# Weights kept across three stage seams: a second pass that begins with the last group, filler matmuls at the ends of stages, and fp32r splits shared out anew

## The chip, the cores and the metric

The kernel runs on one core of one Trainium2 chip. The metric is the device time in microseconds (us) of one launch. TensorE is called PE in the rows, VectorE DVE, ScalarE ACT, GpSimd POOL, SyncE SP (it only issues transfers). PEld is PE's weight load.

## The reference

One decoder layer is run over a prompt of 2048 tokens (width 1024) and over 8 single-token samples, all in fp32. What matters here:

```python
h = rmsnorm(x) @ w_in         # queries, keys, values, z of three branches and three gates, in groups of 512 columns
o_fox = fox_prompt(...)       # 8 heads x 64: softmax(q k^T * scale + c_t - c_s), causal, times v
o_hg, state = hgrn2(...)      # 4 heads x 128: gated linear recurrence, a state of 128x128 per head
o_mem = mem_attn(q, mk, mv)   # 4 heads x 128 over 256 memory tokens; mk, mv = rmsnorm(mem) @ w_mk, w_mv
ya, yb, ym = (o_fox*silu(z)) @ w_pa, (rmsnorm(o_hg)*silu(z)) @ w_pb, (o_mem*silu(z)) @ w_pm
y = rmsnorm(x + (sigmoid(ga)*ya + sigmoid(gb)*yb + sigmoid(gm)*ym) @ w_o)
```

The samples attend to a paged cache of 2048 past tokens each and have their own recurrent state. Keys, values, log gates, memory keys and values and states are outputs too.

## The kernel before

Six stages follow each other. Each is a block: all engines must have ended the one before they start the next.

1. `normalise_and_project`: norms of 16 prompt tiles of 128 tokens (and 2 memory tiles), turned by PE; the first group of columns, `hi`.
2. `project_and_decode`: seven groups (`DENSE`: fq, mq, hf, hq, hz, fz, mz) over two passes of the tokens. A pass keeps 8 of the 16 token tiles in `x_both`. A unit is one tick: 24 matmuls of 512 columns (8 slices of the contraction, 3 products each). A group is 8 ticks, so there are 14 groups and 112 ticks. The other 8 token tiles are loaded over the first during the last group of pass one. Beside it the samples' attention over their cache (`Decode`, laid out by tick numbers), their recurrence and the forget gates run.
3. `recur_prompt`: the recurrence, 64 chunks `n`; five lead-in steps (`AHEAD`) prepare the first units.
4. `attend_prompt`: forgetting attention, a hand-written list `steps`.
5. `attend_memory`.
6. `merge_and_finish`: branch projections, gates, `w_o`, final norm.

A product in fp32 is made of three fp32r matmuls: a number is split in a high part (a cast to fp32r) and a low part (number minus high part). For each weight slice of 128x512 somebody has to load a raw slice, cast it (`..._hi`) and subtract (`..._lo`). In stage 2 POOL does all three for all 104 slices (`split_slice`, with `RAWS` = 2 raw buffers); the slices live in a ring of 16 places (`ring_hi`, `ring_lo`), the last four of which serve the cache's values during decoding.

Ten column groups (fk, fv, six halves of gates, and mk, mv of the memory) are not done in stage 2: the `Filler` spreads their matmuls through stages 3 to 5, to keep PE at work while the others compute. `fill.begin` cuts them into slots: a group has 400 matmuls (16 tiles by 24, and 16 more for the samples), mk and mv have 48 each. A group's eight weight slices are split by POOL as soon as the last tile of the group before has used them (`Filler.split_slice`). Each tile of tokens comes by a load `fill_x` of 1 MB, two buffers. `MATMULS` sets the counts: 1600 in the recurrence (four whole groups, over 134 slots), 100 + 1396 in the attention, 200 in the memory stage.

PE, ACT, DVE and POOL run their own lists in order; a wait holds whatever stands behind it on that engine. At the start of stage 3 POOL builds the masks before it releases `consts`, for which PE and DVE wait; at the start of stage 4 PE waits for `consts_ready`. In stage 6 the 16 slices of `w_o` pass through the same four raw buffers as the branch weights: SP loads, ACT casts, DVE subtracts, all between tile 0's branches and its `mixed` turn.

## Time and profile before

| | us |
|---|---|
| median of 3 runs | 3064.44 (3054.81 to 3074.55) |
| the profiled execution | 3058.63 |
| its span, first to last instruction | 3056.9 |
| PE busy in the span | 2802.7 (92%) |
| DVE busy | 1583.8 (52%) |
| ACT busy | 1036.8 (34%) |
| POOL busy | 811.6 (27%) |
| mean granted PE clock | 0.961 |

Busy is the time in which an instruction of the engine ran. A group of rows with "[x <-y]" at the end of a row tells that the engine was idle for x us before that row's first instruction and that y ended the wait. The granted clock is 1.00 at 2.4 GHz and 0.50 at 1.2 GHz; a stretch's number is its mean.

### The profile page before, as it was taken

To read this page: it belongs to the slowest core of one execution; us is meant where nothing else is said; L and a number is where in the kernel's file an instruction comes from. 1 tells how busy PE (TensorE), PEld (TensorE's weight loads), DVE (VectorE), ACT (ScalarE), POOL (GpSimd) and SP (SyncE) were. 2 spreads that over 40 slices of the span, in tenths; PEclk is the share of its full clock that TensorE was granted. 3 is DMA by queue.
4 is the path that set the end of the run, shared out by engine and by line. 5 is a ranking of instruction groups with operands and counts; after the bars stand their busy time and mean duration, and the time that the engine had idled before them with its cause. 6 is when DMAs were issued, how large, how long until landed. Compare 5 with 4: busy or idle time off the path is not lost. (4 is left out here: it accounts for less than half of the span.)

```text
span 3056.9 us, 38630 instructions
## 1 busy us (share of the span) xinstructions
PE 2802.7 (92%) x13880; PEld 2295.1 (75%) x13880; DVE 1583.8 (52%) x3023; ACT 1036.8 (34%) x1972; POOL 811.6 (27%) x846
## 2 busy tenths in 40 slices
PE   7899998999995989999779999999999977999998
PEld 5678776667774878787658888888887865888887
DVE  5415676343443446556426665666664545444544
ACT  2211111332321334344225555555554234232322
POOL 6058885344244252533350020020020000000000
PEclk9999998999997999999889999999999998999999
DMA  5587778566544657666575455554443545433331
GB/s 168 222 257 230 233 249 277 186 176 185 174 136 143 200 194 244 205 219 200 176 223 155 138 147 160 156 160 142 139 139 114 198 170 173 131 107 117 116 109 49
DMA packets 292430, 528.44 MB, mean 173 GB/s; under 512 B 110398, under 2 KB 135551, under 8 KB 270991
## 3 DMA queue, kind: packets, MB, share of 16 engines
q1 hardware_dynamic: 239967, 408.13, 42.5%
q0 software_dynamic: 16656, 53.36, 6.0%
q10 hardware_dynamic: 35616, 64.47, 5.5%
q8 instruction: 111, 1.82, 0.2%
q14 instruction: 80, 0.66, 0.1%
HBM read 413.19 MB, written 112.68 MB: 172 GB/s over the span
## 5 line engine op out<-in xcount | busy, mean ns | idle before, releaser
L2452 PE MATMUL fill_out<-fill_w_hi,fill_x 128*128 128x512 f32 x2112 | 739.1, 414 | 94.3 <-POOL fill_w_lo L2545 45.0
L2452 PEld LDWEIGHTS fill_out<-fill_w_hi,fill_x 128*128 128x128 f32 x2112 | 393.7, 193 | 174.4 <-POOL fill_w_lo L2545 58.9
L2452 PE MATMUL fill_out<-fill_w_lo,fill_x 128*128 128x512 f32 x1056 | 438.1, 415 | 0.0
L461 DVE TENSOR_TENSOR fox_pt_lo<-fox_turned,fox_pt_hi 128x512 fp32r<-128x512 f32 (+1 forms) x320 | 194.8, 609 | 157.1 <-ACT fox_pt_hi L408 155.3
L2086 ACT ACTIVATE in_stage<-in_out 128x512 f32<-128x512 f32 (+1 forms) x119 | 70.9, 597 | 593.7 <-PE in_out L99 546.3
L408 ACT ACTIVATE fox_pt_hi<-fox_turned 128x512 fp32r<-128x512 f32 (+1 forms) x320 | 170.1, 531 | 300.8 <-PE fox_turned L358 299.1
L447 DVE CUSTOM_DVE_ANT_0 fox_probs<-fox_scores,fox_bias 128x512 f32<-128x512 f32 (+2 forms) x320 | 187.5, 608 | 93.1 <-PE fox_scores L347 50.6
L2543 POOL CAST fill_w_hi<-fill_raw 128x512 fp32r<-128x512 f32 x80 | 51.5, 644 | 678.5 <-PE fill_out L2463 643.5
L2452 PEld LDWEIGHTS fill_out<-fill_w_lo,fill_x 128*128 128x128 f32 x1056 | 204.6, 194 | 30.5
L97 PE MATMUL in_out<-x_first,ring_hi 128*128 128x512 f32 x512 | 201.0, 393 | 7.4 <-POOL ring_lo L2007 7.4
L99 PE MATMUL in_out<-x_first,ring_hi 128*128 128x512 f32 x512 | 200.5, 392 | 0.0
L98 PE MATMUL in_out<-x_first,ring_lo 128*128 128x512 f32 x512 | 200.5, 392 | 0.0
L358 PE MATMUL fox_turned<-ident,fox_probs 128*128 128x128 f32 x1088 | 172.7, 274 | 9.1 <-ACT fox_probs L399 8.9
L97 PE MATMUL mf_out<-mf_w_hi,mf_t_hi 128*128 128x512 f32 x408 | 166.4, 408 | 1.5 <-DVE mf_w_lo L2919 1.5
L99 PE MATMUL mf_out<-mf_w_lo,mf_t_hi 128*128 128x512 f32 x408 | 161.3, 395 | 0.0
L98 PE MATMUL mf_out<-mf_w_hi,mf_t_lo 128*128 128x512 f32 x408 | 161.1, 395 | 0.0
L358 PEld LDWEIGHTS fox_turned<-ident,fox_probs 128*128 128x128 f32 x1088 | 128.5, 140 | 39.4 <-ACT fox_probs L399 14.6
L97 PE MATMUL in_out<-ring_hi,x_first 128*128 128x512 f32 x384 | 154.1, 401 | 4.0 <-POOL ring_lo L2007 4.0
L399 ACT ACTIVATE fox_probs<-fox_probs,fox_neg_most 128x128 f32<-128x128 f32 (+15 forms) x128 | 153.2, 1197 | 11.4 <-ACT fill_stage L2479 9.3
L98 PE MATMUL in_out<-ring_hi,x_first 128*128 128x512 f32 x384 | 152.7, 398 | 0.0
L99 PE MATMUL in_out<-ring_lo,x_first 128*128 128x512 f32 x384 | 152.7, 398 | 0.0
L2007 POOL TENSOR_TENSOR ring_lo<-in_raw,ring_hi 128x512 fp32r<-128x512 f32 x104 | 146.7, 1410 | 8.7
(356 smaller groups left out, 5932.8 us busy)
## 6 DMA issues: line engine op xcount, KB each, us to landing
fill_x<-x_tiles SPq DMA_DIRECT2D x132, 1024.0 KB, 5.4
dc_slot<-in_cache_fox_k_dram SPq DMA_DIRECT2D x128, 256.0 KB, 3.9
dc_slot<-in_cache_fox_v_dram SPq DMA_DIRECT2D x128, 256.0 KB, 3.1
in_raw<-in_w_in_dram POOLq DMA_DIRECT2D x104, 256.0 KB, 4.0
plain<-fill_stage ACTq DMA_DIRECT2D x96, 256.0 KB, 5.4
mf_gate<-plain SPq DMA_DIRECT2D x96, 256.0 KB
turned<-in_stage ACTq DMA_DIRECT2D x64, 256.0 KB, 3.9
fill_raw<-in_w_in_dram POOLq DMA_DIRECT2D x64, 256.0 KB, 3.0
```

The costliest lines, as they stand in the source:

```text
L97: pe.matmul(out, a[0], b[0], start=first, stop=False)
L98: pe.matmul(out, a[1], b[0], start=False, stop=False)
L99: return pe.matmul(out, a[0], b[1], start=False, stop=last)
L358: last = pe.transpose(bank_of(st)[:, t * P:(t + 1) * P], probs_of(4 * q + t, j * P, (j + 1) * P), core.ident[:])
L399: act.activation(probs_of(i, 0, (i + 1) * P), probs_of(i, 0, (i + 1) * P), ACT.Exp, bias=neg_most[:, slot:slot + 1], accum_out=row_sum[:, ...
L408: act.activation(pt_hi[:, zeta % PT_SLOTS, skip:BANK], bank_of(st)[:, skip:BANK], ACT.Copy).then_inc(hi_ready, 1)
L447: dve.tensor_tensor_reduce(probs_of(i, c * BANK, c * BANK + width), scores[s % S_BANKS][:, 0:width], bias[:, c * BANK:c * BANK + width], 1 ...
L461: dve.tensor_tensor(pt_lo[:, b, skip:BANK], bank_of(st)[:, skip:BANK], pt_hi[:, b, skip:BANK].bitcast(F32), ALU.subtract).then_inc(turned_ ...
L2007: pool.tensor_tensor(lo, raw[m % RAWS][:], hi.bitcast(F32), ALU.subtract).then_inc(split, 1)
L2086: act.activation(stage[s][0:rows_, :], out[e % OUTS][0:rows_, :], how, scale=scale).then_inc(sigmoid_ready if kind == "silu" else taken, 1)
L2452: ins = pe.matmul(self.out[n % self.OUTS][:], x, w, start=(k == 0 and term == 0), stop=(ends and term == 2))
L2543: pool.tensor_copy(self.w_hi[:, k, :], self.raw[n % self.RAWS][:]).then_inc(self.split, 1)
```

## The change

- Pass two of stage 2 takes its groups in the order mz, fq, mq, hf, hq, hz, fz. The first of them is the group that pass one ended with, and its split weights stay where they are. Pass two waits for each token tile by itself.
- In place of the group that is no longer loaded, the first Filler group's weights (fk) are split at the end of stage 2, into the upper half of the ring. That half is now two tensors, `keep_hi` and `keep_lo`, which outlive stage 2 and serve the Filler as its weights.
- Casts in stage 2 go from POOL to ACT (`high`), and POOL keeps the loads and the subtractions (`low`). There are three raw buffers. In pass one two slices are taken per tick in ticks 0 to 3 of a group, where one per tick stood in ticks 0 to 7. In the recurrence the Filler's casts go to ACT as well.
- Ticks of the decode's softmax steps and of the forget gates move later by one to three.
- Stage 3: PE no longer waits for constants at its start, POOL builds the masks after the first unit's gates, SP loads the first token tile before anything else. 96 filler matmuls stand at the end, in four slots between the last output pieces.
- Stage 4: PE's wait for constants stands at the first score; head 1's queries and values are loaded later; 10 and 12 filler matmuls frame the last `back`. Stage 5 begins with 16 filler matmuls and has one more slot.
- The filler matmuls are shared out anew, and mk, mv come after the third gate half.
- Stage 6: POOL loads, casts and subtracts `w_o` through two buffers that are parts of `gains`; the final gain is loaded behind it.

The diff, cut to its core:

```diff
 attend_prompt
-    steps += [("out", *quads[-1]), ("back", *quads[-1])]
+    TAIL = FILLS + 2 * FH * J_HEAD
+    steps += [("out", *quads[-1]), ("fill", TAIL), ("back", *quads[-1]), ("fill", TAIL + 1)]
...
-                        if st[0] in ("queries", "values") and st[2] == QUADS - 1 and st[1] + 1 < FH:
+                        if st[0] in ("queries", "values") and st[2] == QUADS - 1 and 1 <= st[1] < FH - 1:
                             (load_queries if st[0] == "queries" else load_values)(st[1] + 1)
+                        if st == ("score", 0, 0, 0):
+                            load_queries(1)
+                            load_values(1)
...
-                pe.wait_ge(consts_ready, 1)
...
+                        if (h, i, c) == (0, 0, 0):
+                            pe.wait_ge(consts_ready, 1)
 recur_prompt
-        fill.begin([0] * 2 * SPLITS + fill.spread(matmuls, 2 * (len(chunks) + AHEAD - SPLITS)))
+        fill.begin(fill.spread(matmuls, 2 * (len(chunks) + AHEAD)) + fill.spread(last_matmuls, TAIL), True)
...
+                fill.sync_start(sp)
                 load_unit(0)
+                fill.sync_next(sp)
+                load_unit(1)
                 load_v(0)
-                fill.sync_start(sp)
-                for u in range(1, HH):
+                for u in range(2, HH):
                     load_unit(u)
...
-                    if n + AHEAD < SPLITS:
-                        fill.gpsimd_first(pool, n + AHEAD, SPLITS)
+                    if n == 2 - AHEAD:
+                        build_masks()
...
+                def tail(piece):
+                    for slot in tail_slots(piece):
+                        fill.tensor(pe, slot)
 attend_memory
-        fill.begin(fill.spread(matmuls, NT))
+        fill.begin([first_matmuls] + fill.spread(matmuls - first_matmuls, NT + 1))
...
+                fill.tensor(pe, 0)
                 pe.wait_ge(kv_loaded, 32)
 Decode.tensor
-            if m == 2:
+            if m == 3:
                 pe.wait_ge(self.spread_ready, a + 1)
 project_and_decode
+    group_at = [*range(G), G - 1, *range(G - 1)]
+    load_at = [n if n < G else n - 1 for n in range(N + 1)]
...
+        def split_at(m):
+            n, k = first_use[m // KT], m % KT
+            if ring_before[m] is not None and last_use[ring_before[m] // KT] == n - 1:
+                return n * U - 1
+            return (n - 1) * U + (k // 2 if n < G else k)
...
+                def low(m):
+                    hi, lo = w_ring.at(ring_at[m])
+                    pool.wait_ge(cast, m - KT + 1)
                     pool.tensor_tensor(lo, raw[m % RAWS][:], hi.bitcast(F32), ALU.subtract).then_inc(split, 1)
-                    if m + RAWS < N * KT:
-                        pool.wait_ge(split, 2 * (m - KT) + 2)
+                    if m + RAWS < SLICES:
+                        pool.wait_ge(split, m - KT + 1)
                         load_raw(m + RAWS)
...
-                    if n == G and u % 4 == 0:
-                        pe.wait_ge(x_loaded[u // 4], 64)
+                    if n == G:
+                        pe.wait_ge(x_loaded[u], 16)
...
+                def high(m):
+                    act.wait_ge(raw_loaded[m % RAWS], 16 * ((m - KT) // RAWS + 1))
+                    ring_free(act, m)
+                    act.activation(w_ring.at(ring_at[m])[0], raw[m % RAWS][:], ACT.Copy).then_inc(cast, 1)
+
                 for t in range(TICKS):
+                    for m in range(KT, SLICES):
+                        if split_at(m) == t and t % U == U - 1:
+                            high(m)
                     for e in events_at(t):
                         evict(e)
                         if e >= 1:
                             store(e - 1)
+                    for m in range(KT, SLICES):
+                        if split_at(m) == t and t % U < U - 1:
+                            high(m)
 Filler
+    def high_by_scalar(self, act, n):
+        self.wait_slice(act, n)
+        act.activation(self.w_hi[:, n % KT, :], self.raw[n % self.RAWS][:], ACT.Copy).then_inc(self.cast, 1)
 merge_and_finish
+            @block.gpsimd
+            def _(pool):
...
+                for i in range(2):
+                    load(i)
+                for i, (kk, n) in enumerate(last_slices):
+                    at = slice(n * BANK, (n + 1) * BANK)
+                    pool.wait_ge(late_loaded[i % 2], 16 * (i // 2 + 1))
+                    pool.tensor_copy(w_hi[:, kk, at], late_raw[i % 2]).then_inc(late_split, 1)
+                    pool.wait_ge(late_split, 2 * i + 1)
+                    pool.tensor_tensor(w_lo[:, kk, at], late_raw[i % 2], w_hi[:, kk, at].bitcast(F32), ALU.subtract
+                                       ).then_inc(late_split, 1)
+                    if i + 2 < len(last_slices):
+                        pool.wait_ge(late_split, 2 * i + 2)
+                        load(i + 2)
+                pool.wait_ge(late_split, 2 * len(last_slices))
+                pool.dma_start(gains[:], gain.partition_broadcast(P)).then_inc(gains_loaded, 16)
...
-                            pe.wait_ge(w_split, MERGE_W + (n + 1) * KT)
+                            pe.wait_ge(late_split, 2 * (n + 1) * KT)
-MATMULS = {"recur": 1600, "first": 100, "fox": 1396}
+MATMULS = {"recur": 1340, "recur_last": 96, "fox_first": 144, "fox": 1472, "fox_last": [10, 12], "memory_first": 16}
```

Three places in the order of the instructions. The first is POOL's list at the start of the recurrence; `fill_raw` are the Filler's raw slices, `hg_f0` the gates of unit 0. Before:

```order
L2529 DMA fill_raw1<-in_w_in_dram 128x512
L635 MEMSET hg_masks 128x512
...
L647 AFFINE_SELECT hg_masks<-hg_masks 128x128 x4
L649 MEMSET hg_state 128x512
L650 MEMSET hg_ones 128x128
L669 TENSOR_SCALAR hg_f0<-hg_f0,rest,bound 128x512
L672 TENSOR_SCALAR hg_k0<-hg_f0 128x512
L2543 CAST fill_w_hi<-fill_raw0 128x512
L2545 TENSOR_TENSOR fill_w_lo<-fill_raw0,fill_w_hi 128x512
L2529 DMA fill_raw0<-in_w_in_dram 128x512
...
L656 TENSOR_TENSOR hg_level0_0<-hg_b0 128x512
```

And with the change:

```order
L2611 DMA fill_raw1<-in_w_in_dram 128x512
L651 MEMSET hg_state 128x512
L652 MEMSET hg_ones 128x128
L688 TENSOR_SCALAR hg_f0<-hg_f0,rest,bound 128x512
L691 TENSOR_SCALAR hg_k0<-hg_f0 128x512
L675 TENSOR_TENSOR hg_level0_0<-hg_b0 128x512
...
L700 TENSOR_SCALAR hg_leaf_k0<-hg_leaf_k0 128x512
L656 MEMSET hg_masks 128x512
```

The masks stand behind unit 0's differences, and no weight slice is split here. The second place is PE's list at the end of the recurrence (`hg_kv` is the last chunk's update) and the start of the attention. Before:

```order
L846 MATMUL hg_o_sum0<-hg_state,hg_q_run3 128x128
L849 MATMUL hg_kv0<-hg_v1,hg_k_rows1 128x128
L572 UNCONDITIONAL_BRANCH
L303 UNCONDITIONAL_BRANCH
L2452 MATMUL fill_out0<-fill_w_hi,fill_x0 128x512 x2
```

With the change:

```order
L877 MATMUL hg_o_sum0<-hg_state,hg_q_run3 128x128
L880 MATMUL hg_kv0<-hg_v1,hg_k_rows1 128x128
L2528 MATMUL fill_out0<-keep_lo,fill_x1 128x512
L2528 MATMUL fill_out0<-keep_hi,fill_x1 128x512 x2
L2528 MATMUL fill_out0<-keep_lo,fill_x1 128x512
```

96 filler matmuls now stand between the last chunk and the end of the block. The third place is ACT's list in pass one of stage 2, with the change, in ticks 0 and 1 of one group (`in_out` is PE's result, `in_stage` the row to be stored); before, only the evictions and the stores stood there:

```order
L2161 ACTIVATE rest_hi<-in_raw2 128x512
L2161 ACTIVATE rest_hi<-in_raw0 128x512
L2150 ACTIVATE in_stage1<-in_out1 128x512
L2156 DMA turned<-in_stage0 128x512
L2161 ACTIVATE rest_hi<-in_raw1 128x512
L2161 ACTIVATE rest_hi<-in_raw2 128x512
L2150 ACTIVATE in_stage2<-in_out2 128x512
```

Two casts stand between two evictions there.

## Rows read from the trace of the kernel before

**Rows 1.** Busy time by stretch, core 0; the header row names the columns.
```profile
core 0: us, PE busy (x) PEld busy (x) DVE busy (x) ACT busy (x) POOL busy (x), PEclk, DMA share, GB/s
151.00:948.00 797.00, 754.31 (x3291) 589.70 (x3292) 365.90 (x427) 169.29 (x295) 427.82 (x397) 0.97 0.65 204
948.00:1009.00 61.00, 26.04 (x74) 17.22 (x72) 19.39 (x19) 11.69 (x19) 43.30 (x62) 0.61 0.60 205
1009.00:1507.00 498.00, 472.95 (x2487) 397.52 (x2486) 272.97 (x439) 192.79 (x415) 177.46 (x193) 0.97 0.62 207
1507.00:1600.00 93.00, 49.76 (x197) 38.16 (x196) 34.84 (x68) 20.80 (x44) 57.02 (x70) 0.76 0.70 209
...
2363.00:2380.00 17.00, 6.24 (x24) 4.95 (x23) 3.11 (x9) 0.66 (x3) 0.00 (x0) 0.60 0.75 273
...
2494.00:2570.00 76.00, 36.17 (x139) 27.86 (x138) 41.02 (x65) 35.89 (x59) 0.00 (x0) 0.76 0.68 229
```

**Rows 2.** PE's waits: line, waited for, us in total, times, longest.
```profile
PE fill_out L2452 <- POOL fill_w_lo L2545: 45.0, 24, 7.3
...
PE mf_turned L2802 <- DVE mf_m_lo L2911: 15.5, 1, 15.5
PE in_out L97 <- POOL ring_lo L2007: 11.4, 8, 2.1
PE mem_turned L966 <- DMA mem_v<-out_dram: 9.4, 1, 9.4
...
PE in_out L2037 <- POOL ring_lo L2007: 8.6, 4, 4.1
PE in_small L1676 <- DVE dc_spread L1614: 8.2, 1, 8.2
```

**Rows 3.** PE's timeline, start of the recurrence: start, us, line, tile.
```profile
966.99 1.19 PE L2452 MATMUL fill_out<-fill_w_hi,fill_x 128*128 128x512 f32 x2 [18.59 <-DMA fill_x<-x_tiles]
...
1009.00 0.83 PE L826 MATMUL hg_att<-hg_level 128*128 128x128 f32 x6
```

**Rows 4.** POOL's timeline, start of the recurrence.
```profile
955.24 0.54 POOL L635 MEMSET hg_masks<- 128x512 f32 x1
...
977.90 3.09 POOL L656 TENSOR_TENSOR hg_level<-hg_b 128x512 f32<-128x512 f32 x3
```

**Rows 5.** DVE's timeline: one product of the recurrence, twice.
```profile
979.75 3.57 DVE L772 TENSOR_TENSOR hg_level<-hg_level,hg_k 128x256 f32<-128x256 f32 x1 [9.87 <-ACT hg_level L711]
...
1020.76 0.42 DVE L772 TENSOR_TENSOR hg_level<-hg_level,hg_k 128x256 f32<-128x256 f32 x1 [0.28 <-ACT hg_level L711]
```

**Rows 6.** PE's timeline at the start of the attention.
```profile
1534.37 1.22 PE L2452 MATMUL fill_out<-fill_w_hi,fill_x 128*128 128x512 f32 x2 [26.85 <-POOLq L229]
...
1535.82 1.05 PE L2452 MATMUL fill_out<-fill_w_hi,fill_x 128*128 128x512 f32 x2
...
1537.10 1.05 PE L2452 MATMUL fill_out<-fill_w_hi,fill_x 128*128 128x512 f32 x2
...
1540.42 0.62 PE L2452 MATMUL fill_out<-fill_w_hi,fill_x 128*128 128x512 f32 x2
...
1541.12 0.62 PE L2452 MATMUL fill_out<-fill_w_hi,fill_x 128*128 128x512 f32 x2
...
1554.77 1.11 PE L334 MATMUL fox_turned<-ident,fox_k_raw 128*128 128x128 f32 x4 [6.63 <-DMA fox_k_raw<-out_dram]
```

**Rows 7.** POOL's groups of instructions in 205 to 470 us: count, busy, mean ns, idle.
```profile
L1527 POOL TENSOR_TENSOR dc_slot<-dc_slot,dc_q 128x1024 f32<-128x1024 f32 x47 | 113.5, 2423 | 30.1 <-DMA dc_slot<-in_cache_fox_k_dram 22.6 <-DMA dc_q<-rows_s 6.9
L2007 POOL TENSOR_TENSOR ring_lo<-in_raw,ring_hi 128x512 fp32r<-128x512 f32 x39 | 54.1, 1388 | 3.1
L2005 POOL CAST ring_hi<-in_raw 128x512 fp32r<-128x512 f32 x38 | 33.8, 888 | 0.0
L1993 POOL DMA_DIRECT2D in_raw<-in_w_in_dram x38 | 21.9, 575 | 11.3 <-POOL ring_lo L2007 11.3
```

**Rows 8.** The chain that ended last, one transfer of w_o: start, us.
```profile
2544.15 5.72 DMA mf_res<-in_w_o_dram
```

More of the change, by code:

```diff
@@ L365, in _ @@
                         fill.tensor(pe, slots_of(st)[1])
-                    if kind == "out" and st is steps[-2]:
+                    if kind == "out" and (h, rest[0]) == quads[-1]:
                         while pending:
@@ L480, in _, with recur_prompt @@
                         dve.sem_inc(turned_used, 1)
-def recur_prompt(nc, core, queries, gates, values, z_hg, gain, gated, state_out, fill, matmuls, needed):
+def recur_prompt(nc, core, queries, gates, values, z_hg, gain, gated, state_out, fill, matmuls, last_matmuls, needed):
     CH = 4
@@ L857, in extra, with tail, attend_memory @@
                     fill.tensor(pe, slots_of(n)[1])
-                walk(nothing, pairs, sums, nothing, extra)
-def attend_memory(nc, core, queries, mem_k, mem_v, z_mem, gated, last, fill, matmuls, needed):
+                def tail(piece):
+                    for slot in tail_slots(piece):
+                        fill.tensor(pe, slot)
+                walk(nothing, pairs, sums, nothing, extra, tail)
+def attend_memory(nc, core, queries, mem_k, mem_v, z_mem, gated, last, fill, matmuls, first_matmuls, needed):
     ST = NM // P
@@ L1069, in extra, with __init__, at, kept @@
                 def extra(u):
-                    fill.scalar(act, u)
+                    fill.scalar(act, u + 1)
                     paged.scalar(act, u)
+                fill.scalar(act, 0)
                 walk(score, nothing, nothing, extra)
+class Ring:
+    def __init__(self, keep, rest):
+        self.keep, self.rest = keep, rest
+    def at(self, place):
+        return [t[:, place % KT, :] for t in (self.keep if place >= KT else self.rest)]
+    @staticmethod
+    def kept():
+        return [*range(KT, 2 * KT)]
 class SampleRows:
@@ L2778, in _ @@
                     if t == 0:
-                        for i in range(MERGE_W, len(slices)):
-                            load_w(i)
                         load_x(0)
```

315 lines of the change are left out of this document (175 added, 140 removed).

## Prediction

> **What bounds the kernel now.** I read the busy time by stretch first. PE is busy 92% of the span, and in every stretch it is the engine with the most work; nothing else comes near it except POOL in the second stage. The change removes no matmul and adds none, so its worth is PE's lost time: time in which PE is idle, and time in which it works at the lower clock. The stretches show where that lies [rows 1]. Idle is length less busy. At a mean clock c, PE was at half speed for 2(1-c) of the stretch, and half of what it did in that time is lost.
>
> - Stage 2 (151 to 948): idle 797 - 754.3 = 43 us; at half speed 0.06 x 797 = 48 us, of which I take some 35 as busy, so 17 lost: 60 in all.
> - Start of the recurrence (948 to 1009): idle 35 us, half speed 0.78 x 61 = 48 us, so of the 26 busy some 17 were at half speed, 9 lost: 44.
> - Rest of the recurrence (1009 to 1507): idle 25 us, half speed 0.06 x 498 = 30 us, up to 12 lost: 37.
> - Start of the attention (1507 to 1600): idle 43, half speed 0.48 x 93 = 45, of that some 18 busy, 9 lost: 52.
> - Start of the memory stage (2363 to 2380): idle 11, 2 lost: 13.
> - Start of the merge (2494 to 2570): idle 40, half speed 36 with 14 of it busy, 7 lost: 47.
>
> That is 253 us in six places. Next the list of PE's waits, which says who ends them [rows 2]: the Filler's splits on POOL lead with 45.0 us, then w_o's turn at the merge (15.5), the ring of stage 2 (11.4 + 8.6), the memory stage's load (9.4), the decode's spread (8.2). The timelines give the two largest single gaps: 18.59 us before the first filler matmul and 26.85 us before the attention's first [rows 3, 6].
>
> A matmul's price comes from the timeline: three filler matmuls start every 1.28 us at the half clock and every 0.70 us at the full one, 0.43 and 0.23 each; after the gap of 26.85 us PE was at half speed for some 5 us, 3 of them lost [rows 6].
>
> **The change, term by term.**
>
> *A, stage 2.* POOL works through 1.26 cache products a tick at 2.42 us and, per slice, 0.89 + 1.39 + 0.58 us [rows 7]: 3.05 + 2.86 = 5.9 us, against a tick of 24 x 0.23 = 5.5. So POOL falls behind in pass one, and PE meets it at group seams. With the cast on ACT (busy 169 of 797 us [rows 1]; 104 casts at no more than POOL's 0.89 add up to 93) POOL has 3.05 + 1.97 = 5.0 us a tick: it keeps up. In pass two four slices a group wait for their place; without the cast they pass in 8 us and not 11.4. I take 15 of the 20.0 us on the ring as gone. The spread is asked for a unit later: 5.5 of its 8.2 us. The clock gives back 5. Against it I set 5 us for the new tie of POOL to ACT (first rival). Saved 20, from 0 to 32. That group mz stays saves no work: fk's eight slices are split instead, and they lie beside stage 2's matmuls.
>
> *B, start of the recurrence.* Before, PE reached the first chunk at 1009.0 [rows 3] with six filler slots of 11.9 behind it, 71 matmuls, 16 us of work in 61. Now ten slots of 9.7 lie there, 97 matmuls, 22 us. Nothing of them waits for a split. PE waits only for the first tile, which SP now issues first; the block's first POOL work stands at 955.24 [rows 4], and a transfer of a few us (the longest price I have is 5.72 for 256 KB [rows 8]) puts the start at about 960. 960 + 22 + 3 for the clock is 985. Is unit 0 ready by then? Its differences began at 977.90, after the masks and four slices [rows 4]. Now only the gates, their logarithm and the running sum precede them, and they can stand at 966, end at 972, with the products behind them by about 980. So PE is 24 us earlier and 26 matmuls (6 us) further: saved 30, from 20 to 36.
>
> *C, rest of the recurrence.* Three group seams lie here before and after. A slice costs POOL 1.97 instead of 2.86 us. But ACT now stands in line for the raw slices with its other copies behind it, and with 9.7 matmuls a slot where 11.9 stood, a chunk lasts 1 us less, so the seam's slices have less time. Half of the idle time (12 us) and 4 of the clock: saved 16, from 0 to 25.
>
> *D, start of the attention.* 96 matmuls (22 us) fill the gap of 26.85. The constants no longer stand before PE. What is left is the step from block to block, 5 us. The third key block waited 6.63 us [rows 6]; its load stood on SP behind head 1's queries and values, which now come later: 2 left. Of the idle 43 the remaining 10 belong to mk and mv, whose splits had to come within 48 matmuls at 11 a slot. They move to the middle of the attention, where a slot has 2.3: 3 left. With 3 for the clock, 13 stay of 52: saved 39, from 30 to 45.
>
> *E, memory stage.* 10 + 12 + 16 matmuls, 8.7 us, go into waits of 11 us: saved 8, from 5 to 10.
>
> *F, start of the merge.* The wait of 15.5 us goes [rows 2], since w_o no longer stands between the branches and the `mixed` turn on SP, ACT and DVE, and 3 us of clock with it. POOL's 16 slices take (5.72 + 0.89 + 1.39 + 0.58)/2 = 4.3 us each with two buffers: 69 us from 2500, so 2569. PE wants the second half at the end of tile 1's branches, some 22 us after the turn that now comes at 2546: 2568. It just fits. But w_o's 4 MB now run beside the branch weights, in a stretch where the DMA engines are already busy 68% [rows 1]: 8 us back. Saved 11, from -10 to 18.
>
> Sum: 20 + 30 + 16 + 39 + 8 + 11 = 124 us. The profiled execution had 3058.6, the median is 3064.4 (0.2% more, within the runs' 20 us). 3064 - 124 = **2940 us**. The last tick of stage 6, stage 1 and the middle of the attention keep their time.
>
> **Rivals.**
>
> *POOL tied to ACT and ACT to PE (15%).* A tick's casts stand behind its eviction, so POOL can take them only when PE has finished the unit. In ticks 0 to 3 of a group POOL then has 2 x 1.97 + 3.05 = 7.0 us for a tick of 5.5 [rows 7], and the cache products behind it come late, then DVE's reductions, then its share of the evictions. Against it: PE has four banks, so three ticks of grace, and ticks 4 to 7 need only 3.05. If it bites, 24 ticks at 1.5 us or more is 40 us: A turns from +20 to -20, 2980 us.
>
> *DVE beside POOL (12%).* One product took 3.57 us beside POOL's work and 0.42 a little later [rows 5]. At the merge's start DVE has 24 subtractions of two SBUF operands on the path, and POOL had nothing there; now it has 16 casts and 16 subtractions, 16 x 2.28 = 36 us. If each of the 24 waits for 1 us on average, F is -13: 2964 us. The Trainium skill ("SBUF — State Buffer", SBUF: two separate sides) says that GpSimd and a DVE instruction with two SBUF inputs hold their common port by turns, for a whole instruction. By that rule alone the sum would be F = -13 as here; the trace shows such a stretch in one place and DVE undisturbed in most, so I leave it a rival.
>
> *The first unit sets the start of the recurrence (10%).* If unit 0 is ready only at 1000, since its chain through four engines has other waits than POOL's masks, PE idles 15 us there: the change then does not do what it says at this seam, B is 15, 2955 us.
>
> *Slower (3%).* The late slices' casts stand before the eviction of the group's last tick, and each waits for its raw slice, which waits for POOL's subtraction three slices before. If ACT is thus held at each of the 13 group seams until PE's banks are full, each seam costs PE a wait. From 124/13 = 9.5 us a seam on the kernel is not faster; before, such seams cost 20.0/12 = 1.7 us [rows 2]. With 12 us a seam it would be 3095. Speaks against it: four slices of 5.72 us transfers in three buffers are no more than some 12 us in all, and PE has three ticks (16 us) of grace.
>
> **How the numbers follow.** The forecast's mechanism has 55% (2900 to 2965), the three rivals on the faster side 37%, slower 3%, and 5% is for what I do not see. The range of 8 in 10 reaches to the first rival and to the terms' better ends, 2900 to 2990. One per cent is about what can be told from no change, here 31 us: faster by more than that 94%, within 3%, slower 3%.
>
> **What would show it.** B: the first chunk's `hg_att` 35 to 40 us after stage 2's last matmul, not 61. D: filler matmuls right after the last `hg_kv`, and no gap over 6 us before the attention. A: waits of PE on the ring under 5 us; the first rival would show as PE waiting for ACT's eviction (`taken`) or for decode steps in pass one. C: waits on `fill_w_lo` under 15 us in all, perhaps some on `hg_k_rows`. F: no wait on `mf_m_lo`, and `mf_fin` not waiting for POOL; the second rival shows as DVE's `mf_w_lo` well above 0.7 us. The mean clock should rise from 0.961 to about 0.98. The prediction fails if the stage lengths do not shrink where the waits have gone: then PE was waiting there for something that comes next in time, and the largest of those is the loads' own latency.
>
> The clock's share is worked out from rows. The Trainium skill ("TensorE: Matmul & The Clock Gate", HAM oscillation) says that gaps cost twice, once as idle time and once as work at the lower clock; the rows after the gap of 26.85 us agree.

## The result, and the profile after

| | before | changed |
|---|---|---|
| median, 12 runs each, us | 3071.98 (3054.81 to 3080.35) | 3047.12 (3039.97 to 3055.18) |
| ratio | | 0.9923 (95% interval 0.9909 to 0.9936) |
| span of the profiled execution, us | 3056.9 | 3040.4 |
| mean granted PE clock | 0.961 | 0.967 |

The change takes some 25 us off (0.8%), where 124 were forecast. The profiled executions differ by 16.5 us, since that of before was one of its faster ones. PE is busy 2802.5 us in the changed kernel and 2802.7 before; what went is idle time.

Busy time by stage of the changed kernel, cut at the first and last instruction of each stage on PE. In order: stage 2, the way to the first chunk, the recurrence, the way to the attention's first own instruction, the attention, the way to the memory stage, that stage, the way to the merge, the merge. [rows 1] has columns and stretches of before.

```profile
core 0: us, PE busy (x) PEld busy (x) DVE busy (x) ACT busy (x) POOL busy (x), PEclk, DMA share, GB/s
152.20:964.10 811.90, 757.80 (x3292) 591.39 (x3292) 365.38 (x427) 227.52 (x401) 339.39 (x293) 0.96 0.65 200
964.10:1015.80 51.70, 27.68 (x99) 21.87 (x99) 11.55 (x19) 12.36 (x21) 19.20 (x32) 0.74 0.63 229
1015.80:1452.00 436.20, 403.41 (x2205) 343.85 (x2204) 276.24 (x439) 199.03 (x428) 158.82 (x165) 0.97 0.60 202
1452.00:1501.50 49.50, 32.47 (x130) 25.26 (x129) 17.09 (x23) 8.58 (x18) 2.11 (x8) 0.87 0.82 255
1501.50:2349.60 848.10, 818.21 (x4476) 682.36 (x4475) 477.24 (x1332) 417.99 (x764) 118.38 (x142) 0.99 0.51 153
2349.60:2360.20 10.60, 8.19 (x28) 5.94 (x26) 0.86 (x4) 1.20 (x2) 0.00 (x0) 0.84 0.80 283
2360.20:2486.90 126.70, 120.77 (x726) 105.88 (x726) 72.48 (x190) 36.59 (x138) 0.00 (x0) 0.99 0.48 166
2486.90:2495.80 8.90, 0.00 (x0) 0.00 (x0) 1.13 (x4) 0.00 (x0) 1.11 (x2) 0.61 0.48 175
2495.80:3040.50 544.70, 514.86 (x2380) 422.60 (x2380) 275.40 (x455) 163.36 (x260) 40.70 (x47) 0.97 0.38 122
```

Idle is length less busy. With before cut at the same instructions (stage 2 is 797.3 long there, stages 3 to 5 with their ways 1545.9, the merge with its way 562.7):

| term | forecast, us saved | idle before | idle after | measured |
|---|---|---|---|---|
| A, stage 2 | 20 | 42.6 | 54.1 | -14.6 in length |
| B, to the first chunk | 30 | 35.0 | 24.0 | 11.0 idle |
| C, recurrence | 16 | 25.0 | 32.8 | -7.8 idle |
| D, to the attention, and in it | 39 | 26.9 + 32.1 | 17.0 + 29.9 | 12.1 idle |
| E, memory stage | 8 | 9.4 + 1.4 | 2.4 + 5.9 | 2.5 idle |
| B to E in length | 93 | | | 23.1 |
| F, merge | 11 | 49.1 | 38.7 | 9.1 in length |

The lengths sum to 16.5 with 1.1 lost in stage 1. In B to E the idle time fell by 17.8 us and the length by 23.1: PE does the same matmuls there (7664 records for 7662) in 5.4 us less of busy time, since the ways between the stages ran at a granted clock of 0.74, 0.87 and 0.84 where it had been about 0.6. In the forecast's own count, which also took in the matmuls done before the first chunk, B is 8.9 us of length and 26 matmuls more (6 us), 15 in all. PE's waits of the changed kernel, longest totals first, to be held against [rows 2]:

```profile
PE fill_out L2528 <- DMA fill_x<-x_tiles: 47.2, 9, 14.8
...
PE mf_turned L2916 <- DMA mf_g_in<-gated: 20.0, 7, 9.0
PE fill_out L2528 <- ACT fill_stage L2555: 19.8, 3, 9.6
PE fill_out L2528 <- POOL keep_lo L2637: 18.0, 10, 4.6
PE in_wide L1751 <- DVE keep_lo L1596: 9.5, 3, 4.6
PE in_small L1708 <- DVE dc_slot L1615: 9.1, 1, 9.1
PE in_small L1733 <- DVE dc_sums L1674: 8.7, 1, 8.7
PE mf_out L97 <- DVE mf_w_lo L3031: 8.1, 4, 3.1
```

The named waits did go: the ring's 20 us, the 15.5 on `mf_m_lo`, and the Filler's splits fell from 45.0 to 18.0. In their place stand the token tiles (21.1 us in three waits before, 47.2 in nine now), ACT's eviction `fill_stage` (19.8), the decode's steps, and DVE's `mf_w_lo`. So the question of the experiments is: which edit called up which of these, and can it be had without.

### The profile page after: what moved, and what is told of

It reads as the page before. It is cut to its first block and busy times, and to the rows that moved or that the text cites. A ratio compares the mean times of both kernels' runs of the same rounds, so it can differ in the third digit from the quotient of the medians.

```text
span 3040.4 us, 38617 instructions
## 1 busy us (share of the span) xinstructions
PE 2802.5 (92%) x13880; PEld 2295.6 (76%) x13880; DVE 1577.6 (52%) x3007; ACT 1098.7 (36%) x2086; POOL 728.0 (24%) x743
## 5 line engine op out<-in xcount | busy, mean ns | idle before, releaser
L2528 PE MATMUL fill_out<-keep_hi,fill_x 128*128 128x512 f32 x2112 | 739.8, 413 | 87.4 <-DMA fill_x<-x_tiles 47.2
L2528 PEld LDWEIGHTS fill_out<-keep_hi,fill_x 128*128 128x128 f32 x2112 | 391.7, 193 | 160.8 <-issue 36.1
L2528 PE MATMUL fill_out<-keep_lo,fill_x 128*128 128x512 f32 x1056 | 433.8, 411 | 3.9 <-PEq L3215 3.9
L2528 PEld LDWEIGHTS fill_out<-keep_lo,fill_x 128*128 128x128 f32 x1056 | 203.6, 193 | 35.7 <-issue 4.3
L404 ACT ACTIVATE fox_probs<-fox_probs,fox_neg_most 128x128 f32<-128x128 f32 (+15 forms) x128 | 153.2, 1197 | 16.1 <-ACT fill_stage L2555 8.5
L363 PEld LDWEIGHTS fox_turned<-ident,fox_probs 128*128 128x128 f32 x1088 | 128.7, 140 | 37.6 <-ACT fox_probs L404 11.5
L1579 POOL TENSOR_TENSOR dc_slot<-dc_slot,dc_q 128x1024 f32<-128x1024 f32 x54 | 130.7, 2429 | 84.1 <-DMA dc_slot<-in_cache_fox_k_dram 59.7
L2555 ACT ACTIVATE fill_stage<-fill_out 128x512 f32<-128x512 f32 (+1 forms) x140 | 83.0, 593 | 140.7 <-PE fill_out L2528 138.9
L351 PE MATMUL fox_scores<-fox_k_hi,fox_q_both 128*128 128x512 f32 (+2 forms) x320 | 121.2, 379 | 5.2 <-DVE fox_most L452 4.0
L97 PE MATMUL in_out<-rest_hi,x_first 128*128 128x512 f32 x288 | 118.1, 410 | 3.6 <-DVE in_stage L2190 3.6
L2076 POOL TENSOR_TENSOR rest_lo<-in_raw,rest_hi 128x512 fp32r<-128x512 f32 x56 | 73.6, 1313 | 187.8 <-ACT rest_hi L2161 187.2
L319 PE MATMUL fox_o_sum<-fox_pt_lo,fox_v_both 128*128 128x512 f32 (+1 forms) x320 | 117.0, 366 | 0.0
L98 PE MATMUL in_out<-rest_hi,x_first 128*128 128x512 f32 x288 | 116.5, 405 | 0.0
```

Of the source, the lines that this page charges most:

```text
L97: pe.matmul(out, a[0], b[0], start=first, stop=False)
L98: pe.matmul(out, a[1], b[0], start=False, stop=False)
L319: last = pe.matmul(o_sum[:, skip:BANK], v_both[h % 2][:, j, :], p[:, zeta % PT_SLOTS, skip:BANK], start=(j == 0 and m == 0), stop=(j == 4 ...
L351: pe.matmul(out, q_both[:, i * P:(i + 1) * P], k_hi[:, keys], start=True, stop=False)
L363: last = pe.transpose(bank_of(st)[:, t * P:(t + 1) * P], probs_of(4 * q + t, j * P, (j + 1) * P), core.ident[:])
L404: act.activation(probs_of(i, 0, (i + 1) * P), probs_of(i, 0, (i + 1) * P), ACT.Exp, bias=neg_most[:, slot:slot + 1], accum_out=row_sum[:, ...
```

## Experiments on stage 2 (term A)

ACT evicts 119 results there, so the n-th eviction's start on ACT's timeline tells how far a kernel has come. Its lag behind the kernel before, us (a minus is a lead). The first eviction differs already by up to 6 us: stage 2 starts up to 3 us apart, and its first matmuls stood some 0.44 us apart in some executions (before, e1, e5, e8: the half clock) and 0.25 in others (changed). The edits have no part in that, so lags are to be compared with the first row taken off:

| eviction (time before) | changed | e1 | e2 | e3 | e5 | e8 | e9 | e13 | e10 |
|---|---|---|---|---|---|---|---|---|---|
| 1 (156) | -0.3 | 4.1 | 3.6 | 4.9 | 3.5 | 3.6 | -1.1 | -0.2 | 0.2 |
| 8 (203) | 11.1 | 9.9 | 11.8 | 6.8 | 15.5 | 4.5 | 3.9 | 7.6 | 5.3 |
| 32 (334) | 15.4 | 5.8 | 22.1 | 13.9 | 19.9 | 10.4 | 6.8 | 15.4 | 12.7 |
| 48 (431) | 25.5 | 17.7 | 26.1 | 15.7 | 31.9 | 11.7 | 9.4 | 20.4 | 23.4 |
| 52 (455) | 34.2 | 27.9 | 26.1 | 15.5 | 40.9 | 11.5 | 9.2 | 20.4 | 25.0 |
| 64 (558) | 23.7 | 18.8 | 19.0 | 10.0 | 18.7 | -1.2 | -7.0 | 3.7 | 15.9 |
| 112 (910) | 15.8 | 20.8 | 12.4 | 13.1 | 12.1 | 1.5 | -14.0 | -3.0 | 18.5 |

With that done, kernels that share their code up to a point still differ there by up to 4 us (changed and e5, e8 and e9 to eviction 52), so that much is noise. Pass one (to 56) loses up to 34 us; pass two wins back 8 of them from 64 on, the ring's waits.

**e1, casts on POOL; e2, one slice per tick; e3, both.**

```diff
 e1, low(m)
+                    pool.wait_ge(raw_loaded[m % RAWS], 16 * ((m - KT) // RAWS + 1))
+                    ring_free(pool, m)
+                    pool.tensor_copy(hi, raw[m % RAWS][:]).then_inc(cast, 1)
 e2, split_at(m)
-            return (n - 1) * U + (k // 2 if n < G else k)
+            return (n - 1) * U + k
```

> The changed kernel with the 104 casts of stage 2 back on POOL (three raw buffers, two slices per tick in pass one and everything else stay as changed). Theory 1, POOL is tied to ACT: a cast stands behind an eviction, POOL's subtraction waits for the cast, and the log gates' load, the cache products and DVE's reductions behind it come late. Then the gap of 9.1 us at 191 goes, PE's waits of 7 us on in_stage go, the lag of ACT's evictions against the kernel before (11 us at unit 8, up to 34 at unit 52) stays under 8, stage 2 ends 12 to 20 us earlier, and some ring waits (up to 10 us) come back: 3030 to 3038 us. Theory 2, it is the crowding of two slices into each of ticks 0 to 3: POOL now needs 2 x 2.86 + 3.05 = 8.8 us in such a tick of 5.5 instead of 7.0, so the lag grows beyond 34 and the kernel is 10 us slower or more: 3057 or above.

> The changed kernel with one slice per tick in ticks 0 to 7 of pass one, where it has two in ticks 0 to 3; the casts stay on ACT. Theory 1 (tie to ACT): the gap at 191 shrinks but stays (POOL still waits for casts behind evictions), the lag of the evictions stays at 10 to 30 us: 3040 to 3050. Theory 2 (crowding): lag below 10 by unit 52, stage 2 ends 12 to 20 us earlier: 3028 to 3035.

> The changed kernel with both undone: casts of stage 2 on POOL and one slice per tick. Pass one of stage 2 is then as before except for the third raw buffer. Both theories: no lag at unit 8, stage 2 about as long as before (ends by 948 to 952 against 964), 3030 to 3036. If it still ends at 960 or later, neither the tie nor the crowding is the cause, but the moved decode ticks or the order of the second pass.

Measured: e1 3045.8 us, ratio 0.993 (0.9905 to 0.9955); e2 3039.0, 0.9909 (0.9882 to 0.9936); e3 3035.7, 0.9902 (0.9874 to 0.9930). The three intervals overlap with each other and with the changed kernel's 0.9909 to 0.9936, so by the ratios no edit can be told from another, nor any of the three from the changed kernel. The lag gained from eviction 1 to 52, where pass one has lost most, makes a table of two by two:

| lag gained, 1 to 52 | casts on ACT | casts on POOL |
|---|---|---|
| two slices in a tick | 34.5 (changed) | 23.8 (e1) |
| one slice | 22.5 (e2) | 10.6 (e3) |

The tie costs 11 to 12 us in pass one and the crowding 12 to 13, and they add: neither theory is the whole. In pass two it turns, from 64 to 112 the changed kernel and e2 win 8 and 7 us, e1 and e3 lose 2 and 3. At 112 the lags gained are 16.1 (changed), 16.7 (e1), 8.8 (e2) and 8.2 (e3): over the whole stage the place of the casts cancels out, and the crowding costs 8. e3's time came out as expected, but its stage 2 ended at 961.5 and not by 952, which leaves the moved decode ticks or the new order of pass two as a further cause; the row on `dc_sums` is 10.5 us in e3.

**e5, the last sample row.** DVE's timeline at the pass seam, first before, then changed; `sr_part` is the sum of a sample's row that comes by a load, `dc_sums` the softmax sums for which PE waits:

```profile
518.53 2.08 DVE L1622 TENSOR_REDUCE dc_sums<-dc_scores 128x64 f32<-128x1024 f32 x1
...
531.53 0.68 DVE L1127 TENSOR_TENSOR sr_part<-sr_part 8x512 f32<-8x512 f32 x1 [9.43 <-DMA sr_part<-sample]
```
```profile
555.50 0.68 DVE L1178 TENSOR_TENSOR sr_part<-sr_part 8x512 f32<-8x512 f32 x1 [9.41 <-DMA sr_part<-sample]
...
558.32 1.98 DVE L1674 TENSOR_REDUCE dc_sums<-dc_scores 128x64 f32<-128x1024 f32 x1
```

The load is as late in both, but moving `dc_sums` one tick put it behind a stalled instruction. PE's row there is the 8.7 us above.

```diff
 SampleRows.vector, likewise scalar and the store
-            if t == self.tick_of(i) + 1:
+            if t == self.tick_of(i) + 1 + self.delay(i):     # 2 for the last row, else 0
```

> The changed kernel with one edit in stage 2: the last of the sample rows (mz) is summed, gated and stored two ticks later; its load stays. Theory: DVE stood 9.4 us before that row's load, and the reduction dc_sums, which the change moved by one tick, now stands behind it on DVE instead of ahead, so PE's wait moved from dc_spread (8.2 to 2.7 us) to dc_sums (8.7 us, new). Then the wait on dc_sums goes under 2 us and the one on keep_lo behind it does not grow: stage 2 is 7 to 12 us shorter, 3035 to 3040. Rival: the softmax chain itself (spread, exp, sums over ACT and DVE) is late; then 5 us or more stay on dc_sums and the time stays at 3043 or more.

Measured: 3032.6 us, ratio 0.9872 (0.9856 to 0.9889). PE's waits in 500 to 600 of e5:

```profile
PE in_wide L1754 <- DVE keep_lo L1599: 3.3, 1, 3.3
PE in_small L1731 <- DVE dc_spread L1669: 2.1, 1, 2.1
PE in_small L1736 <- DVE dc_sums L1677: 0.4, 1, 0.4
```

8.7 became 0.4 and nothing grew behind it. In the lags it gains 22 us from 52 to 64 where the changed kernel gains 10.5. The median gains more (15 us) than the 8 us of idle time; the profiled execution was the slowest of its four (3043.7 us, no shorter than the changed kernel's 3042.4), so the time rests on the other three launches and 7 us of the gain are not found in a trace.

**e13 and e9, who casts, with the rest mended.** e9 is e8 (below) with the casts of pass two on ACT and those of pass one on POOL; e13 has both on ACT.

```diff
 e9, high(m) on ACT only for slices of pass two
-                        if split_at(m) == t and t % U < U - 1:
+                        if split_at(m) == t and t % U < U - 1 and first_use[m // KT] >= G:
```

> As the kernel with all five edits, but the casts of the second pass of stage 2 stay on ACT, as in the change; those of the first pass are on POOL. Theory: the tie of POOL to ACT costs only where POOL is nearly full, in pass one; in pass two the casts on ACT take the ring waits of 1.1 to 1.9 us at six seams away (8.7 us in the kernel with all five edits). Then ratio to before 0.974 to 0.9755, 2990 to 2996. Rival: the tie costs in pass two as well; 2999 or above.

> As the best kernel so far (2986 us, ratio 0.9725), but with the casts of pass one of stage 2 on ACT too, at one slice per tick. Theory: the tie of POOL to ACT and of ACT to PE's units costs by itself in pass one (the log gates' load comes behind two more casts that wait for evictions, and the cache products shift): 6 to 12 us more, ratio 0.9745 to 0.9765. Rival: at one slice per tick POOL has the 0.9 us per slice back and the tie costs nothing: ratio 0.971 to 0.9735.

Measured: e9 2986.1 us, ratio 0.9725 (0.9705 to 0.9745); e13 3002.1, 0.9769 (0.9755 to 0.9782). Here the tie stands alone: casts on ACT cost 10 us in pass one (a lag of 20.6 against 10.5 gained up to 48) and bring 10 in pass two (from 64 to 112 e9 gains 7.0, e8 loses 2.7). The theory of e13 holds: a cast waits behind an eviction, and `low` waits for the cast. POOL's waits in pass one (152 to 490) of e13 have two rows that e9 has not:

```profile
POOL keep_lo L2081 <- ACT keep_hi L2166: 54.4, 12, 14.4
POOL rest_lo L2081 <- ACT rest_hi L2166: 35.5, 11, 10.8
```

That is 90 us in 23 waits, up to 14.4 us at a time, with whatever stands behind `low` on POOL late by as much. That pass two gains because POOL has little behind it there is argued.

**e10, cache products from POOL to DVE**, e8 with `POOL_SHARE = 2` for 4.

> As the kernel with all five edits, but every second cache product of the decode goes to DVE (36 of 72 where 18 stood); POOL keeps 36. Theory: what is left of pass one's waits (3 to 6 us at four group seams, on ring slices) is POOL's queue; it loses 18 x 2.42 = 44 us of work and DVE gets 18 x 1.22 = 22, so these waits go: 8 to 12 us off, ratio 0.973 to 0.975. Rival: DVE's products wait for POOL's running instruction (they took 1.22 us alone and 3.3 to 7.2 beside it), DVE comes late with rs_state and the evictions' products, and new waits of the same size or more stand there: ratio 0.977 or above.

Measured: 3015.2 us, ratio 0.9816 (0.9793 to 0.9839), 13 us worse than e8 (0.9772). It is the rival's outcome, and half of its mechanism: DVE does come late (PE waited 10.9 us for `rs_state` in 180 to 500, against 4.3 in e8), but not since its products wait for POOL. DVE's products in 200 to 470, e10 and then e8:

```profile
L1584 DVE TENSOR_TENSOR dc_slot<-dc_slot,dc_q 128x1024 f32<-128x1024 f32 x29 | 47.8, 1650 | 90.1 <-DMA dc_slot<-in_cache_fox_k_dram 90.1
```
```profile
L1584 DVE TENSOR_TENSOR dc_slot<-dc_slot,dc_q 128x1024 f32<-128x1024 f32 x16 | 41.6, 2600 | 45.5 <-DMA dc_slot<-in_cache_fox_k_dram 45.5
```

A product got shorter (2.60 to 1.65 us), but DVE now stands 90 us before cache loads instead of 45, with the samples' state and the evictions' products behind it. POOL, on this reading, had served as the engine that may wait; no run isolates it.

## Experiments on the Filler's seams (term C)

ACT's timeline at the second seam of the changed kernel, and PE's row that waits for it:

```profile
1255.01 0.63 ACT L721 ACTIVATE hg_log_f<-hg_f 128x512 f32<-128x512 f32 x1
1260.13 1.26 ACT L2632 ACTIVATE keep_hi<-fill_raw 128x512 fp32r<-128x512 f32 x2 [4.49 <-DMA fill_raw<-in_w_in_dram]
1261.29 0.26 ACT L748 ACTIVATE hg_k_rows<-hg_turned 128x128 f32<-128x128 f32 x1
1261.45 0.59 ACT L2555 ACTIVATE fill_stage<-fill_out 128x512 f32<-128x512 f32 x1
```
```profile
1262.09 1.22 PE L2528 MATMUL fill_out<-keep_hi,fill_x 128*128 128x512 f32 x2 [9.60 <-ACT fill_stage L2555]
```

ACT stands at a raw slice with the eviction behind it. Is ACT's list the cause, or the slices' way?

```diff
 e4, the casts of the recurrence's Filler on POOL
-        fill.begin(... + fill.spread(last_matmuls, TAIL), True)
+        fill.begin(... + fill.spread(last_matmuls, TAIL))
 e6, three raw buffers; e15 is e4 and e6 together
-    RING, STAGES, RAWS, OUTS = 2, 2, 2, 2
+    RING, STAGES, RAWS, OUTS = 2, 2, 3, 2
```

> The changed kernel with the Filler's casts in the recurrence on POOL, as before. Theory: ACT is held at a raw slice (5.5 us from issue to landing) with the eviction of the group's last tile behind it, and PE waits for that bank. Then the two gaps of 9.5 us at 1262 and 1405, which end with fill_stage, go, and waits on keep_lo of 6 to 7 us per seam stand there as before: 10 to 13 us off, 3034 to 3037. Rival: the seam is set by the raw slices' way through two buffers, whoever casts; then the gaps only change their name from fill_stage to keep_lo and the time stays within 4 us of the changed kernel, 3043 to 3051.

> The changed kernel with three raw buffers in the Filler instead of two, casts still on ACT. Theory: a group seam is set by the way of the raw slices (256 KB, 3.0 us to land alone, 5.5 beside other loads) through two buffers, and ACT held at one of them holds the eviction. With a third, the two gaps of 9.5 us drop to 4 or less each and the small ones on keep_lo (4.8 us at the first seam) to 2: 12 to 18 us off, 3029 to 3035. Rival: the order of ACT's list (casts ahead of the eviction) is what counts, and the third buffer gives 0 to 5 us: 3042 to 3047.

> The changed kernel with three raw buffers in the Filler and its casts on POOL in the recurrence. With two buffers the casts on POOL cost 10 us more than on ACT, with ACT's a third buffer saved 18. Theory: both costs are the raw slices' way, so with three buffers it is the same who casts: within 4 us of the kernel with three buffers and ACT's casts, ratio 0.985 to 0.9875. Rival: POOL's work per slice (0.9 + 1.3 + 0.6 us beside the recurrence's own) is the limit then, and it stays 8 us or more above: ratio 0.989 or more.

Measured: e4 3056.6 us, ratio 0.9951 (0.9935 to 0.9966), 9 us worse than the changed kernel (the intervals just touch): my theory fell, and the rival was too mild. e6 3028.8, 0.9862 (0.9844 to 0.9879), 19 us better. e15 3042.0, 0.9892 (0.9876 to 0.9907). PE's waits within the recurrence, two rows each of the changed kernel, e4 and e6:

```profile
PE fill_out L2528 <- ACT fill_stage L2555: 19.8, 3, 9.6
PE fill_out L2528 <- POOL keep_lo L2637: 6.8, 4, 2.2
```
```profile
PE fill_out L2528 <- POOL keep_lo L2637: 30.9, 9, 7.0
PE fill_out L2539 <- ACT fill_stage L2555: 4.6, 3, 2.6
```
```profile
PE fill_out L2528 <- ACT fill_stage L2555: 10.9, 2, 7.6
PE fill_out L2528 <- POOL keep_lo L2637: 6.5, 4, 2.8
```

Two limits lie over each other: the raw slices' way through two buffers, and POOL's work per slice. ACT's casts take the second away (9 us with two buffers, 9 with three: 0.9892 against 0.9862), the third buffer eases the first (19 us with the casts on ACT, of which 10 lie in the recurrence and 7 in the attention, by the stages' lengths; 18 with them on POOL, by the ratios). In e15 25.6 us of waits on `keep_lo` are left in the recurrence. So the casts on ACT were right, and what the change lacked was a buffer. What I can't show is why the same casts on POOL cost 30.9 us in e4 and 19.8 in the kernel before, in the same seams; the shorter slots (9.7 matmuls for 11.9) fit, but no run varied them alone.

## Experiments at the stage starts (terms B and D)

SP's timeline at the start of the recurrence, changed kernel, and the two rows of PE that waited:

```profile
974.08 0.35 SPq L2577 DMA_DIRECT2D fill_x<-x_tiles  x1
...
975.41 0.75 SPq L2577 DMA_DIRECT2D fill_x<-x_tiles  x1
...
984.90 2.27 SPq L603 DMA_DIRECT2D hg_z<-plain  x2
987.21 1.38 SPq L2577 DMA_DIRECT2D fill_x<-x_tiles  x1
```
```profile
978.91 1.22 PE L2528 MATMUL fill_out<-keep_hi,fill_x 128*128 128x512 f32 x2 [14.78 <-DMA fill_x<-x_tiles]
1001.55 1.19 PE L2528 MATMUL fill_out<-keep_hi,fill_x 128*128 128x512 f32 x2 [9.24 <-DMA fill_x<-x_tiles]
```

The third tile (1 MB) is asked for at 987.2, behind 15 loads, and PE has it 14 us later. The transfer rate from 974 to 990, 40 slices:

```profile
GB/s 0 0 184 123 20 348 369 451 492 328 348 348 261 179 164 123 184 261 287 425 430 399 481 410 410 435 388 369 375 409 410 394 358 399 343 399 410 405 445 374
```

It stays near 400 GB/s from the seventh microsecond on: at that rate a tile of 1 MB alone would take 2.6 us (an estimate), and the rest of the 14 us is the queue ahead of it.

```diff
 e7, recurrence: out of SP's start, into extra(n)
+                    if n == 1 - AHEAD:
+                        for u in range(2, HH):
+                            load_unit(u)
+                        sp.dma_start(gains[:], gain.partition_broadcast(P)).then_inc(gains_loaded, 16)
+                        for i in range(2):
+                            load_z(i)
 e7, attention
                     load_values(0)
+                    fill.sync(sp, 0)
                     for n in range(2):
                         load_keys(*quads[n])
```

> The changed kernel with SP's loads in another order at two stage starts: in the recurrence units 2 and 3, the gain and z come behind the third token tile; in the attention the token tile of the first filler slot comes ahead of the keys, the bias and z. Theory: the tile that PE waits for (9.2 us at 1001, 10.7 at 1500) is late because 4 MB and more stand ahead of it on SP's queue while the DMA engines are full, or because SP has not come to it. Then both gaps drop under 3 us each: 12 to 18 us off, 3029 to 3035. Rival: a tile of 1 MB in two buffers cannot keep up with PE's burst of fillers (24 matmuls, 5.6 us a tile) in any order; then the sum of the two gaps stays over 12 us and the time over 3041.

Measured: 3035.8 us, ratio 0.9897 (0.9865 to 0.9928), 8 us, though the interval overlaps the changed kernel's. The trace agrees in size: the 9.24 us became 2.58 + 4.27, the 10.74 us at 1500 became 5.21: 12.1 left of 20.0. Both theories had a part: order was worth 8 us, and the rest, I take it, is the burst itself, since two buffers must be refilled within the 5.6 us that PE needs for a tile. That the burst is the limit is argued, not shown: a third token buffer, 8 KB in a partition, was not tried.

**e14, half the tail**, `"recur": 1388, "recur_last": 48` on e9.

> As the best kernel so far, with 48 instead of 96 filler matmuls behind the last chunk; the other 48 go to the slots between the chunks. Theory: a token tile needs about 6 to 7 us through its two buffers and PE uses it up in 5.6, so of 96 matmuls in a row the second half only runs into waits; the four waits of 1 to 1.7, 3.7 and 5 us at the seam shrink, and nothing is lost: ratio 0.9705 to 0.9735. Rival: the last output pieces need the time of all 96 (DVE and ACT's post), PE idles instead before the attention: 5 to 11 us more, ratio 0.974 or above.

Measured: 2988.0 us, ratio 0.973 (0.9715 to 0.9746): as e9. 48 matmuls serve that seam as well as 96 (idle on the way to the attention 13.1 us against 11.6, in the recurrence 21.6 against 20.7); PE's waits on token tiles stay at 36 us, so the second half of its theory, that they shrink, did not hold.

**e12, masks built first**, as before, in the changed kernel.

> The changed kernel with the masks of the recurrence built at the stage's start again, ahead of the first unit's gates. My step of term B: the masks' way to the end of unit 0's differences brings unit 0 forward, so undoing it costs 5 to 9 us (8.6 us of POOL's work): 3052 to 3056. Rival, from the trace after: POOL waits 7.1 us for the gates' load anyway and PE gets to the first chunk only at 1016, 20 us after unit 0's last product on DVE, held by the token tiles; then it changes nothing: 3044 to 3050.

Measured: 3042.8 us, ratio 0.9901 (0.9879 to 0.9923): not slower. POOL's row in the changed kernel says why, it waits for the gates' load with nothing to do:

```profile
983.54 0.78 POOL L688 TENSOR_SCALAR hg_f<-hg_f,rest,bound 128x512 f32<-128x512 f32 x1 [7.13 <-DMA hg_f<-turned]
```

## The merge alone (term F), and all edits together

e11 is the kernel before with `merge_and_finish` of the changed one.

> The kernel before with one part of the change alone: w_o loaded, cast and subtracted by POOL in stage 6. My term F said 11 us off (15.5 + 3 us gained, 8 lost to the loads beside the branch weights): 3058 to 3064 against 3072, ratio 0.995 to 0.9975. Rival: DVE's subtractions on the path wait beside POOL's work; F is -13, ratio 1.003 or above.

Measured: 3064.7 us, ratio 0.9982 (0.9961 to 1.0003), some 5 us off that can't be told from nothing; in the trace the merge with its way takes 9 us less and 11 us less idle. POOL and DVE do meet. DVE's subtractions to 2575, before and then changed:

```profile
L2919 DVE TENSOR_TENSOR mf_w_lo<-mf_res,mf_w_hi 128x512 fp32r<-128x512 f32 x40 | 27.2, 691 | 19.8 <-ACT mf_w_hi L2864 19.7
```
```profile
L3031 DVE TENSOR_TENSOR mf_w_lo<-mf_res,mf_w_hi 128x512 fp32r<-128x512 f32 x24 | 27.4, 1181 | 7.7 <-ACT mf_w_hi L2978 7.6
```

0.49 us each for 24, half of my rival's price of 1 us, and PE waits 8.1 us for them, where it waited 1.5 before.

**e8** joins e3, e5, e6 and e7.

> The changed kernel with all five edits together: casts of stage 2 on POOL, one slice per tick, the last sample row two ticks later, three raw buffers in the Filler, SP's new order at two stage starts. If the causes are separate their savings add: 11 (both stage 2 edits, measured) + 9 + 15 + 14 = 49 us, 2992 to 3006. If they share one cause, or the next wait stands close behind, it stays above 3012.

Measured: 2998.8 us, ratio 0.9772 (0.9750 to 0.9793). Against the changed kernel's 0.9923 that is 46 us. By their ratios the single runs sum to 49 as well (e3 6, e5 16, e6 19, e7 8), each 4 to 7 us from what I had put in: within the noise the causes are separate and add. With pass two's casts on ACT again (e9) it is 2986.1 against 3068.6 for before in the same comparison, 82 us less, and 0.98 of the changed kernel. It is the best kernel of the study, with e14 level with it.

## Why the prediction failed, step by step

- **A, 35 us off.** The ring's waits went as said. The step that failed is "I set 5 us for the new tie of POOL to ACT": the tie costs 10 to 12 us in pass one (e13, e1, e2), two slices in a tick another 12 to 13, of which 8 are left at the stage's end (e2, e3), and the moved ticks gained 5.5 us on `dc_spread` as forecast and lost 8.7 on `dc_sums` (e5). The tie by itself is paid back in pass two. I priced POOL by its mean per tick and took the moved ticks for harmless where they gave time; I had not looked at what stands ahead of them on DVE. The first rival had this mechanism for pass one, and it showed as I had named it, by waits for decode steps and evictions. That its size nearly fits (-20; -14.6 measured) is partly luck: the `dc_sums` wait is in the measured number and not in the rival.
- **B, 19 us off in idle time, 15 in the forecast's own count.** "PE waits only for the first tile" failed: the third tile was late by 9.24 us, and the first gap is 14.8, not some 12: SP issued its first load 10.0 us after stage 2's last matmul, where it took 5.2 before (953.65 against 948.4). The masks' move (my reason for unit 0 at 980) is worth nothing (e12). Unit 0's products ended at 996.6, not 980: the gates came by a load that landed 7 us after POOL was ready. That did not set the chunk either: PE ran its filler matmuls without a gap from 1001.55 to the chunk at 1015.8. PE got to the chunk 52 us after stage 2, not 37.
- **C, 24 us off.** The granted clock is 0.97 in both, so little of its 4 us can have come. I gave ACT's casts half of the idle time. They do bring 9 us (e4), but the seams had got dearer by more, and their limit, two raw buffers, was not in my sum at all (e6).
- **D, 27 us off.** The gap of 26.85 was filled, and two of 10.7 and 5.4 for token tiles took its place. Moving mk and mv to where a slot has 2.3 matmuls saved none of the 7 us: their waits on the split were 8.9 us before (1507 to 1600) and are 10.4 now (1811 to 1847). A third buffer took 7 us off the attention.
- **E, 5.5 us off**, for a token tile too (3.9 us at 2377).
- **F was right in size** (11; 9 to 11 in the traces, 5 by e11's launches), but by two errors that cancel: PE's waits for `mf_w_lo` grew from 1.5 to 8.1 us, which I had only in a rival, and the loads beside the branch weights did not cost my 8 (the waits on `mf_g_in` are 20.0 us now and were 21.8). I left that rival small since the trace showed such a stretch "in one place"; in the kernel before 11 of DVE's 18 cache products between 219 and 500 took over 2 us, where 1.22 is the least.

The mean granted clock rose from 0.961 to 0.967 and not to some 0.98, since the gaps did not go. My last sentence on what would make it fail named the cause of B to E, the loads' own latency, and I gave it no chance and no price. The range ended 57 us below the measured time, because each rival on the faster side changed a single term, while the true case missed five at once: behind each wait that went stood another, for a load or a buffer in B to E and for a cast or a decode step in A.

The Trainium skill ("SBUF — State Buffer", SBUF: two separate sides) says that the loser at the common port of GpSimd and DVE waits for the whole instruction. The rows of stage 2 below agree and go further: there DVE waited through three of POOL's instructions.

## What to carry to other kernels

Before a gap is filled with work, ask how fast that work's own inputs can come: here PE used up a tile in 5.6 us, and even the best kernel kept 36 us of waits for tiles. Before an instruction is moved one place on an in-order engine, read what stands just ahead of it and how long that waits. An engine that waits for transfers is a poor place for work on which others wait, even if its busy share is low; price a new wait by its worst tick and not by the mean.

## What was not expected of the hardware

A DVE product of two SBUF operands takes 1.22 us with POOL idle and took 6 us more beside POOL, which went from one instruction to the next; DVE twice, and then POOL, of the changed kernel:

```profile
487.76 1.22 DVE L1579 TENSOR_TENSOR dc_slot<-dc_slot,dc_q 128x1024 f32<-128x1024 f32 x1 [4.41 <-DMA dc_slot<-in_cache_fox_k_dram]
464.19 7.24 DVE L1579 TENSOR_TENSOR dc_slot<-dc_slot,dc_q 128x1024 f32<-128x1024 f32 x1 [0.65 <-DMA dc_slot<-in_cache_fox_k_dram]
```
```profile
464.32 4.78 POOL L1579 TENSOR_TENSOR dc_slot<-dc_slot,dc_q 128x1024 f32<-128x1024 f32 x2
469.06 1.28 POOL L2076 TENSOR_TENSOR rest_lo<-in_raw,rest_hi 128x512 fp32r<-128x512 f32 x1
```

DVE ended 1.1 us after POOL's third instruction in a row, about one product's time: it did not get in between two of them. Two more products went the same way: 7.14 us at 289.62 beside three of POOL's instructions and 6.17 at 415.21 beside two; each ended 1.1 us after the last of them.

The step from stage 2 to stage 3 took 10 us from PE's last matmul to SP's first load in all kernels with pass two's casts on ACT (964.1 to 974.1 in the changed one) and 5 us with them on POOL (949.9 to 955.2 in e8), with no transfer under way in the last 5 or more of the longer one. The last stores were issued at the same distance behind the last matmul in both. Its cause stays open; no run was made for it. It would be worth 5 us to e9, and it is 5 us of what term B missed.
